# Decode attention: the value sums of a group accumulate in one held PSUM bank, the turnings of the prompt use the other two

## The reference, cut to what matters

```python
def stick_breaking(q, k, v, sb_bias, q_pos, k_pos):
    z = jnp.einsum('bqhd,bkhd->bhqk', q, k) * (HEAD_DIM_SB ** -0.5)
    z = z + sb_bias[None, :, None, None]
    mask = k_pos[None, :] < q_pos[:, None]
    log_1mb = jnp.where(mask, jax.nn.log_sigmoid(-z), 0.0)
    suffix = lax.cumsum(log_1mb, axis=3, reverse=True) - log_1mb
    a = jnp.where(mask, jnp.exp(jax.nn.log_sigmoid(z) + suffix), 0.0)
    return jnp.einsum('bhqk,bkhd->bqhd', a, v)
...
k_past = cache_k[i][page_table].reshape(dec_b, past, N_HEADS_SB, HEAD_DIM_SB)
v_past = cache_v[i][page_table].reshape(dec_b, past, N_HEADS_SB, HEAD_DIM_SB)
k_all = jnp.concatenate([k_past, k], axis=1)
v_all = jnp.concatenate([v_past, v], axis=1)
o_sb = stick_breaking(q, k_all, v_all, sb_bias[i], q_pos_s, k_pos_s)
```

## Time and profile before

| | us |
|---|---|
| median of 3 runs | 3110.92 (3110.59 to 3111.39) |
| profiled execution, its time | 3110.72 |
| its span, first to last instruction | 3108.7 |
| PE busy | 3046.2 (98% of the span) |
| DVE busy | 2029.9 (65%) |
| ACT busy | 1638.2 (53%) |
| mean granted clock of TensorE | 0.995 |

### The profile page before, as it was taken

The page is one execution under the profiler, slowest core; times in us unless marked ns, Lnnn a source line. Parts: engine busy times, 40 slices in busy tenths (PEclk is TensorE's granted clock), DMA queues, the critical chain, the costliest instruction groups (busy, mean ns, idle before and its releaser), DMA issues.

```text
span 3108.7 us, 51907 instructions
## 1 busy us (share of the span) xinstructions
PE 3046.2 (98%) x18572; PEld 2808.4 (90%) x18572; DVE 2029.9 (65%) x2725; ACT 1638.2 (53%) x2359; POOL 147.7 (5%) x277
## 2 busy tenths in 40 slices
PE   8999999799999989999999999999999999999998
PEld 6888888677777769999999999999999999999998
DVE  4222443779977987774777747777477774778745
ACT  5444311899999975443444434444344443444433
POOL 0000000222222200000000000000000000000000
PEclk9999999999999999999999999999999999999999
DMA  5324456766666645434453335434355333543432
GB/s 184 98 94 137 119 151 169 195 158 174 197 162 166 178 129 160 117 112 118 147 149 115 116 114 151 147 113 118 112 155 148 112 115 114 155 122 112 116 115 76
DMA packets 609904, 422.83 MB, mean 136 GB/s; under 512 B 40857, under 2 KB 566082, under 8 KB 609698
## 3 DMA queue, kind: packets, MB, share of 16 engines
q1 hardware_dynamic: 568676, 318.24, 36.0%
q0 software_dynamic: 20544, 67.19, 7.5%
q10 hardware_dynamic: 20512, 35.17, 3.2%
HBM read 367.26 MB, written 53.25 MB: 135 GB/s over the span
## 4 chain that ended last, share of the span: by engine, by line
PE 63%; DVE 0%; issue 0%; DVEq 0%; ACT 0%; ACTq 0%
PE pf_acc L60 21%; PE pf_acc L58 20%; PE pf_acc L59 20%; PE pf_ps_t L1710 1%; PE pf_ps_sum L1649 0%; PE pf_ps_sum L1658 0%; PE pf_ps_sum L1663 0%; PE pf_ps_t L1720 0%; PE pf_ps_t L1781 0%; DVE late_ssum L1988 0%; DVE late_u L1978 0%; DVEq L1586 0%; DVE late_c L2056 0%; DVE pf_h L2182 0%; ACT late_sq L1809 0%
## 5 line engine op out<-in xcount | busy, mean ns | idle before, releaser
L1802 ACT ACTIVATE late_w_hi<-ahead_raw 128x1024 fp32r<-128x1024 f32 x439 | 463.8, 1057 | 549.7 <-PE pf_acc L60 545.8
L60 PE MATMUL pf_acc<-pf_x_hi,late_w_lo 128*128 128x416 f32 x2080 | 734.1, 353 | 0.0
L58 PE MATMUL pf_acc<-pf_x_hi,late_w_hi 128*128 128x416 f32 x2080 | 733.1, 352 | 0.0
L59 PE MATMUL pf_acc<-pf_x_lo,late_w_hi 128*128 128x416 f32 x2080 | 726.0, 349 | 0.0
L1972 DVE TENSOR_TENSOR late_w_lo<-ahead_raw,late_w_hi 128x1024 fp32r<-128x1024 f32 x439 | 536.3, 1222 | 269.5 <-ACT late_w_hi L1802 268.7
L58 PE MATMUL pf_acc<-late_f_hi,late_w_hi 128*128 128x416 f32 x1280 | 453.7, 354 | 5.8 <-DVEq L2195 5.8
L60 PE MATMUL pf_acc<-late_f_hi,late_w_lo 128*128 128x416 f32 x1280 | 452.5, 354 | 0.0
L59 PE MATMUL pf_acc<-late_f_lo,late_w_hi 128*128 128x416 f32 x1280 | 447.9, 350 | 0.0
L59 PEld LDWEIGHTS pf_acc<-pf_x_lo,late_w_hi 128*128 128x128 f32 x2080 | 390.8, 188 | 7.9 <-issue 1.6
L58 PEld LDWEIGHTS pf_acc<-pf_x_hi,late_w_hi 128*128 128x128 f32 x2080 | 390.5, 188 | 3.7 <-issue 1.6
L60 PEld LDWEIGHTS pf_acc<-pf_x_hi,late_w_lo 128*128 128x128 f32 x2080 | 390.0, 187 | 2.3
(11 more groups left out here) (238 smaller groups left out, 4060.6 us busy)
## 6 DMA issues: line engine op xcount, KB each, us to landing
ahead_raw<-in_w_up_dram SPq DMA_DIRECT2D x220, 512.0 KB, 3.9
ahead_raw<-in_w_down_dram SPq DMA_DIRECT2D x80, 512.0 KB, 4.0
high_pages<-in_cache_k_dram POOLq DMA_DIRECT2D x128, 256.0 KB, 4.0
ahead_raw<-in_w_out_dram SPq DMA_DIRECT2D x40, 512.0 KB, 5.4
ahead_raw<-in_w_ple_gate_dram SPq DMA_DIRECT2D x40, 512.0 KB, 4.0
high_pages<-in_cache_v_dram POOLq DMA_DIRECT2D x64, 256.0 KB, 3.7
at_kT<-in_cache_v_dram POOLq DMA_DIRECT2D x64, 256.0 KB, 5.2
ahead_raw<-in_w_down_dram SPq DMA_DIRECT2D x40, 384.0 KB, 3.5
```

The source lines that it names most:

```text
L58: nc.tensor.matmul(out, stat_hi, mov_hi, start=first, stop=False)
L59: nc.tensor.matmul(out, stat_hi, mov_lo, start=False, stop=False)
L60: return nc.tensor.matmul(out, stat_lo, mov_hi, start=False, stop=last)
L1802: nc.scalar.activation(w_hi[k % 4][:, :], raw[k % 4][:, :], ACT.Copy).then_inc(hi_split, 1)
```

## The change

The bank of a fill is no longer its number modulo three, but comes from a small plan `place`: the bank that has been idle longest, except that the first sum of a group takes a bank and keeps it (`held`) to the last of the 16, with all sums in it. The matmuls of the sums start the bank at page 0 only and accumulate after that. ACT's copies and DVE's copy and adds go; DVE's multiply with the mask reads the bank and is what empties it (`sample_own`), at the place on DVE where the mask stood before. The turnings of the prompt use the two other banks meanwhile.

```diff
@@ -982,6 +982,22 @@
+    place, used, oldest = {}, [0] * 3, [0, 1, 2]
+    held = None
+    for key in order:
+        if key[0] == "sum" and key[2]:
+            place[key] = place["sum", key[1], 0]
+        else:
+            bank = [b for b in oldest if b != held][0]
+            place[key] = bank, used[bank]
+            used[bank] += 1
+            oldest.remove(bank)
+            oldest.append(bank)
+            if key[0] == "sum":
+                held = bank
+        if key[0] == "sum" and key[2] == PAGES - 1:
+            held = None
+
     with ExitStack() as ctx:
...
@@ -1000,7 +1016,7 @@
         v_new, aT_new, a_new, merge = spare[0:4 * PB, 576:1088], spare[0:4 * PB, 1088:1216], spare[:, 1216:1232], spare[:, 1232:1248]
-        own, stage = beta_s[:, 0:BANK], [beta_s[:, (n + 1) * BANK:(n + 2) * BANK] for n in range(3)]
+        own = beta_s[:, 0:BANK]
         aT_s = rest_s[:, 0:KEYS].rearrange("p (k t) -> p k t", k=PAGES)
...
@@ -1012,7 +1028,7 @@
         z_ready, b_done, product_done, a_done = (m.sem(n) for n in ("z_ready", "b_done", "product_done", "a_done"))
-        o_ready, o_out, bias_made, rest_zeroed, summed = (m.sem(n) for n in ("o_ready", "o_out", "bias_made", "rest_zeroed", "summed"))
+        o_ready, o_out, bias_made, rest_zeroed = (m.sem(n) for n in ("o_ready", "o_out", "bias_made", "rest_zeroed"))
         filled, emptied = m.sem("filled"), [m.sem(f"emptied{b}") for b in range(3)]
...
@@ -1024,11 +1040,11 @@
         def bank_of(key):
-            return ps_t[fill_at[key] % 3]
+            return ps_t[place[key][0]]
...
-            return emptied[fill_at[key] % 3]
+            return emptied[place[key][0]]
...
@@ -1036,7 +1052,7 @@
             for b in range(3):
-                counts = [fill_at[key] // 3 + 1 for key in keys if fill_at[key] % 3 == b]
+                counts = [place[key][1] + 1 for key in keys if place[key][0] == b]
                 if counts:
...
@@ -1142,10 +1158,10 @@
-                    n = fill_at[key]
-                    if n >= 3:
-                        pe.wait_ge(emptied[n % 3], n // 3)
-                    return ps_t[n % 3]
+                    bank, before = place[key]
+                    if before:
+                        pe.wait_ge(emptied[bank], before)
+                    return ps_t[bank]
...
@@ -1251,10 +1267,10 @@
                         pe.wait_ge(page_loaded[page_slot(g, 1, k, bi)], 16 * page_loads(g, 1, k, bi))
-                    bank = claim(("sum", g, k))
+                    bank = claim(("sum", g, k)) if k == 0 else bank_of(("sum", g, k))
                     for bi in range(PB):
                         last = nc.tensor.matmul(bank[32 * bi:32 * bi + 32, :], aT_s[:, k, 32 * bi:32 * bi + 32], slots[page_slot(g, 1, k, bi)],
-                                                start=True, stop=k < PAGES - 1, tile_position=(0, 32 * bi))
+                                                start=k == 0, stop=False, tile_position=(0, 32 * bi))
                     if k == PAGES - 1:
...
@@ -1344,12 +1360,6 @@
                             .then_inc(emptied_by(key), 1)
-                    if U_SUM <= u < U_MIX:
-                        key, n = ("sum", g, u - U_SUM), PAGES * g + u - U_SUM
-                        if n >= 3:
-                            act.wait_ge(summed, n - 2)
-                        wait_filled(act, key)
-                        nc.scalar.activation(stage[n % 3], bank_of(key)[:, :], ACT.Copy).then_inc(emptied_by(key), 1)
                     if u == U_MIX:
...
@@ -1463,19 +1473,14 @@
-                def sample_sums(g, u):
-                    if U_SUM <= u < U_MIX:
-                        n = PAGES * g + u - U_SUM
-                        wait_emptied(dve, ("sum", g, u - U_SUM))
-                        if u == U_SUM:
-                            nc.vector.tensor_copy(own, stage[n % 3]).then_inc(summed, 1)
-                        else:
-                            dve.wait_ge(summed, n)
-                            nc.vector.tensor_tensor(own, own, stage[n % 3], ALU.add).then_inc(summed, 1)
-                        if u == U_MIX - 1:
-                            dve.wait_ge(summed, n + 1)
-                            nc.vector.tensor_tensor(own.rearrange("p (h d) -> p h d", h=8), own.rearrange("p (h d) -> p h d", h=8),
-                                                    row_head[:, :].unsqueeze(2).to_broadcast([P, 8, 64]), ALU.mult).then_inc(owned, 1)
+                def sample_own(g, u):
+                    if u == U_MIX - 1:
+                        key = ("sum", g, PAGES - 1)
+                        wait_filled(dve, key)
+                        nc.vector.tensor_tensor(own.rearrange("p (h d) -> p h d", h=8), bank_of(key)[:, :].rearrange("p (h d) -> p h d", h=8),
+                                                row_head[:, :].unsqueeze(2).to_broadcast([P, 8, 64]), ALU.mult).then_inc(owned, 1)
+                        dve.wait_ge(owned, g + 1)
+                        dve.sem_inc(emptied_by(key), 1)
...
@@ -1491,7 +1496,7 @@
                         for unit in product_units(t - 1, g):
-                            sample_sums(*unit)
+                            sample_own(*unit)
                     if has(t - 1):
...
```

## The result

The changed kernel takes 3121.2 us (median of 7 runs, 3117.06 to 3122.39), where the kernel before takes 3110.73 beside it (7 runs, 3110.1 to 3112.51). The ratio is 1.0031, 95% interval [1.0021, 1.0042]: slower by 10.5 us, 0.3%. The forecast was 3118.5 in a range of 3114.5 to 3121.0, so the direction and the stops that it rests on held, and the time came out at the upper edge, 0.2 us past it. A second measurement (E9) gave 3119.06 (9 runs, 3117.18 to 3121.15) against 3110.56, ratio 1.0025 [1.0015, 1.0035].

What follows compares the result with a forecast made beforehand. The prediction took PE to bound the kernel, busy 98% of the span. Three terms of 0, stops of 4.2 and 1.75 us and 1.7 us of half clock made +7.65 us: 3118.5 us, range 3114.5 to 3121.0.

Steps and rivals of the forecast that it cites:

- What is taken away: In the decode sums: ACT's copies (19.4 us) and DVE's adds (20.6 us) lie beside a never-waiting PE, worth 0.
- The sums and the mask: In the decode sums: accumulating in the bank and reading the mask's input from it cost the same as now, 0.
- Two banks: Turnings during the sums: with two banks they still find ACT's copies done in time; 0, upper bound 1.5 us.
- rival (e): In the sums: two banks bind, short waits of 1.5 us and one more clock fall, 3120 to 3121.7; chance 0.05.
- The added wait: Behind each group's last sum: PE stops until DVE's mask releases the held bank, 4.2 us and 1.75 us.
- The clock: Behind the first stop: PE's clock falls to half, a loss of 1.7 us; none behind the second.
- (a): The forecast: both stops and the clock, 3118.5, on its own 3117.3 to 3119.7; chance 0.56.
- (c): Key stage: shorter PE waits for ACT give back one to two thirds of the loss, 3113 to 3116.5; chance 0.13.
- (b): Behind the last sums: both stops come but the clock holds, 3116.9; chance 0.13.
- (d): Behind the last sums: DVE doesn't catch up, stops of 8.5 and 7 us with half clock, 3129.8; chance 0.06.
- (f): In the sums: DVE, not PE, is the bound, so steps get shorter, 3098.8; chance 0.04.
- (g): Behind the last sums: the bank is released in time and nothing else changes, 3110.9; chance 0.03.

Runs made afterwards that it cites:

- E9: The changed kernel again, without any edit, for a second measurement and profile; 3119.06 us, ratio 1.0025 against the kernel before.
- E1: The changed kernel, but the held bank stays reserved until the mix instead of going to a turning behind the last sum; 3110.88 us, ratio 1.0003 against the kernel before.
- E4: The kernel before, with a second DVE operation of the same shape behind each of the 30 adds; 3128.31 us, ratio 1.006.
- E10: The changed kernel, but ACT copies the held bank to SBUF right behind the last sum and DVE applies the mask there; 3112.71 us, ratio 1.0007.
- E6: The changed kernel with DVE's mask moved ahead of the weights of its step; 3112.85 us in one run, 3114.95 in ten runs of the same kernel.
- E2: As E1, but in group 0 the held bank goes to the turning behind the last sum; 3117.53 us, ratio 1.0025 against the kernel before.
- E7: E1 with a unit of the keys every 1.6 granules instead of 1.5, a sum every 1.5 instead of 1.875; 3112.38 us, ratio 1.0009.
- E5: As E1, but in group 1 the held bank goes to the turning behind the last sum; 3112.84 us, ratio 1.0011 against the kernel before.
- E8: E1 with a unit of the keys every 1.75 granules and a sum every 1.25; 3127.78 us, ratio 1.0056 against the kernel before.

## Why the prediction held, and where it missed

**What is taken away: 0. Shown**, by the changed kernel (PE's shift is 0.37 us at 742 and 0.39 at 824) and by E1. The thing that I said would show it, "every PE row should stand where it stands now, to 0.1 us", holds inside the sums. The 0.4 us ahead of them are 0.7 us from a half-clock stretch at 577 us, less what PE was early before it. The stretch came behind a wait of PE for ACT of 2.07 us, the same that left the clock at 1.00 in the earlier trace rows. What the prediction didn't say is how thin the cover was on the other side; E4 measures it.

**The sums and the mask: 0. Shown** by E1. The mask out of the bank takes 0.68 us.

**Two banks: 0. Shown** by E1, in which they last even longer. No short waits appear at the five tight places, and rival (e) is out. For the rule of the Trainium skill ("TensorE: Matmul & The Clock Gate", section "A second HAM failure mode: psum-queue depth-cycling"), by which small idles between groups of matmuls lower the clock again and again: this trace shows no such idles with two banks in turn, 82.06 of 82.06 us busy at a granted clock of 1.00, and the clock doesn't move in E1 for 590 us (554 to 1145), both stretches of sums among them.

**The added wait: 4.2 and 1.75. Measured 4.14 and 1.65.** The steps hold too. DVE waits for ACT's sigmoid (1.59 us), has its 7.11 us of scans and weights, and begins the mask at 827.85, where the prediction's 827.46 with the shift of 0.39 lies. The release and PE's start took 0.11 us behind the mask's end, for which I allowed 0.15. Undoing it in parts gives the same: E10 leaves 0.7, E6 1.67, E1 nothing.

**The clock: 1.7 forecast, 3.5 measured. This is the term that was mis-sized.** Behind the first stop it cost 2.1 us (2.05 and 1.8 in the other two profiles), inside the 1.6 to 2.7 that I had bounded. Behind the second I took nothing, because the 1.75 us forecast is less than a stop of 2.07 that had left the clock alone in the earlier trace rows; there it cost 1.4 us. The clock also fell sooner than forecast, at 826.4 us, while PE still stood, and not from the resume on. One row that didn't fall was no bound: the same 2.07 us did lower it in the profile after, and the 1.65 us did so in two profiles of three. The step failed by taking a length of stop as a threshold, from a single row on each side.

**What the sum left out.** By its shifts the changed kernel has 5.9 us of stops and 3.5 of half clock, 9.4 us, which gives 3120.3. The rest of what was measured, on either side (10.5 us in the first measurement, 8.5 in E9), is of the size of what single executions differ by: the half-clock stretches elsewhere, and the end of the kernel, which is 3.3 to 3.4 us behind the start of the last matmul in five profiles (the kernel before, E2, E4, E6, E7) and 4.8 to 5.6 in six (both of the changed kernel, E1, E5, E8, E10). The prediction had only the former, as "a microsecond either way". Two of its bounds don't follow from their own terms: (a)'s upper end would be 3110.9 + 5.95 + 2.7 + 1 = 3120.6 instead of 3119.7, and (c)'s thirds give 3112.9 to 3116.0. Neither changes the forecast.

**The rivals.** (b) has the stops without the clock, 3116.9: excluded in both profiled executions of the changed kernel, though E5 and E6 show it for stops under 2 us. Four executions without a profile took 3117.1 to 3117.9, so for single ones it stays open. (c): nothing is given back, since PE's waits for ACT at the keys stay at 5.4 us in 8 and the shift stays at 6.71 from 840 to 1115; the 0.9 us after the attention are a shorter half-clock stretch. (d): DVE does catch up. (f): E1 excludes it, since no row of PE moves inside the sums when 20.6 us of adds are gone. (g): the stops exist.

## What to carry to other kernels

A bank or buffer that is held over many uses costs at the moment it is given back: look who empties it, what stands before that in the same engine's order, and which fill claims it next. Here three tenths of a percent hung on the choice of the next bank, and leaving the bank out of the rotation until a consumer that waits anyway left no cost that could be measured.

Work taken off engines that run beside the bound was worth nothing here, even off one that was 98% busy in the stretch. But measure the cover in both directions: the engine that gave nothing when relieved of 20.6 us took 18.5 us from the bound when given as much more.

When a stop of the bounding engine is costed, add the clock with a wide bound, and read from more than one execution whether it falls.

## What the runs showed of the hardware

TensorE's granted clock went from 1.00 to 0.50 (2.4 to 1.2 GHz) behind PE's stops as follows. Stop of 4.14 us: fell in three of three profiles. Stop of 1.65 us: fell in two of three. Stops of 1.67 and 0.87 us (E6): not. Stops of 0.7 us (E10): not. The wait of 2.07 us for ACT at about 576, which nine profiles have alike: fell in four (both of the changed kernel, E4, E5), not in five (the kernel before, E1, E2, E6, E10). The same program point with the same wait thus gives both. Other waits at which it fell: 2.10, 3.35 and 4.21 us in E4, 2.47 us in E8. In E7 two shorter waits of 0.67 and 1.13 us end at 573.8 and 576.0, and the clock fell there too. A fall cost PE 1.8 to 2.1 us behind the stop of 4.14, 1.4 behind that of 1.65, and 0.7 at 577: there PE had lost 1.6 us by 579.3, but its next wait for ACT, 0.83 us in the kernel before, was gone.

The end of the kernel has two forms. In the traces of E1, E8 and both of the changed kernel DVE waits 1.7 or 1.8 us in its last rows for a store of the output to land (in E5 and E10 1.1 and 1.0 us for another store, `out_y_sample_dram`), which it doesn't in the kernel before. One of DVE's waits in the last 20 us, in E1 and then in E9:

```profile
DVE late_u L2061 <- DMA out_y_prompt_dram<-late_u: 1.7, 1, 1.7
```

```profile
DVE late_u L2061 <- DMA out_y_prompt_dram<-late_u: 1.8, 1, 1.8
```

It makes the span 1.3 to 2.3 us longer. It comes in profiles with and without stops, but in neither of the two of kernels without a held bank, and what sets it is open.
